# Maximum products on the array's row halves, and expert rows added back while the last tiles run

## The chip, the cores and the metric

The kernel runs on one core of a Trainium2 chip. The metric is the device time of one execution in microseconds (us), as the median of three runs. TensorE (PE) multiplies, with its weight loads shown as PEld; VectorE (DVE), ScalarE (ACT) and GpSimd (POOL) work on vectors; SyncE (SP) only issues DMAs here.

## The reference

One decoder layer over 1,024 tokens of width 1,024, in float32: RMSNorm, one input projection, three groups of attention heads side by side, the output projection, and a mixture of experts, then a last RMSNorm.

```
s_cmp = einsum(qh, k_cmp) * scale - slopes * dist_c      # C: compressed blocks, 8 heads
o_slc: softmax over selected blocks (16 of 16: causal)   # X: 8 heads
o_win: softmax over a band of 512 keys                   # Y: 8 heads
s = qh.kh * scale + (cum[q] - cum[k])                    # F: forgetting heads, 4
attn = p[:, :, 0] - lam_full * p[:, :, 1]                # D: differential heads, 4 x 2 maps
x = x + concat(o_a, o_b, o_c) @ w_out
eid = grp * EXPERTS_PER_GROUP + top_idx                  # two experts for each token
out = out + (silu(h @ w_gate[e]) * (h @ w_up[e]) * gate[:, e]) @ w_down[e]    # e = 0..31
return rmsnorm(x + out, norm_final)
```

## The kernel before

**Projection.** 16 groups of 128 columns are projected transposed, each value split in a high and a low half in fp32r, and the halves are stored in DRAM as `T_d`. This stage is the first 300 us.

**Attention.** `Plan` makes 36 units: for each of eight heads X, C, Y, then four F, then eight D. A unit's score matrix is cut in pieces of one block of 128 keys by up to four blocks of queries. Time is cut in 123 slots. A slot of PE holds up to three pieces of scores (`scores`), three maximum products of a later unit (`max_pass`, six slots ahead), at some slots the transpose of a row of shifts (`shift_T`), and the value products (`values`) of the slot before. A maximum product multiplies a block of queries by up to four blocks of keys, in one matmul over all 128 rows of the array: for X, Y and F the upper 64 rows hold the low half of q against the same k. DVE takes the maximum of each row of it (`maxima`); the maxima, negated, go back over SP's queue as one more row of the operand `Q2` (`shift_row`), so that the exponential of the scores can't overflow. Three PSUM banks take turns for the maximum products. In F units a piece on the diagonal gets a second small matmul (`identr` by `trimr`) that masks it. Value products load 64 columns of weights at a time, onto the two column halves of the array.

SP loads a unit's operands with `load_unit`: six DMAs for X, Y and F (64 rows of `T_d` each) and six of 32 rows for D. It does so two full units ahead, once the unit before has ended its scores (`s_ready`), since the buffers take turns. Between these, from the ninth full unit on, SP also writes seven blocks of zeros to `Y_d` (`zero_rows`, the rows of expert tiles that aren't run), and from the fifth on it loads the output weights (`wraw`).

**Experts.** 34 tiles of 96 token rows (32 experts and two tiles of overflow) run one after the other. In the round of tile n PE does the up product of n, the transposes of n+1, and the down product of n-1. DVE does `m_gate(n)` (with the copy `m_x(n+1)` of the transposed rows inside it), then `m_out(n-1)`. ACT stores each tile's result to `Y_d`. The weights take turns in five buffers; a tile's load is issued when the tile five before it has ended.

**End.** When all tiles are stored, POOL gathers for each of eight blocks of tokens its first and its second expert's row from `Y_d` (16 indirect DMAs, L921), DVE adds them weighted (L1775), takes the roots (`k_roots`, L1760 to L1766), and scales the rows (`k_final`, L1769); SP stores them (L749).

Of the kernel before, what the change touches and what calls it, by code (L numbers as in the profile page):

```python
# [24 lines left out]
P = 128  # L25
NT = SEQ // P
KC = D // P
HD = 64
# [14 lines left out]
NROWS = NTILES * CAP  # L43
# [20 lines left out]

class Unit:
# [6 lines left out]
    def __init__(self, kind, head, u=0):  # L72
# [6 lines left out]
        self.m = []  # L79
        for t in range(NT):  # L80
            for c, k in enumerate(range(lo(t), t + 1, 4)):
                self.m.append((t, c, k, min(4, t + 1 - k)))
# [16 lines left out]
class Plan:  # L99
# [4 lines left out]
    def __init__(self):  # L104
# [28 lines left out]
        early[0].m_use, early[0].tp_use = list(range(12)), 12  # L133
# [67 lines left out]
def program(nc, a, out):  # L201
# [5 lines left out]
    with ctx:  # L207
# [93 lines left out]
        identr, trimr = (at(n, [P, P], f32r, ZB + 60 * KB + 512 * k) for k, n in enumerate(("identr", "trimr")))  # L301
        pt = at("pt", [P, 6, 512], f32, ZE + 12 * KB)
# [4 lines left out]
        zrow = at("zrow", [P, D // 4], f32, ZE + 32 * KB)  # L307
# [24 lines left out]
        slf, shi, slo = (ri(n, [P, 2, NT]) for n in ("slf", "shi", "slo"))  # L332
# [30 lines left out]
        y1 = at("y1", [P, NT, D], f32, ZD)  # L363
        y2 = at("y2", [P, NT, D], f32, ZD + 32 * KB)
        gfin = at("gfin", [P, D], f32, ZC)
# [10 lines left out]
        Y_d = nc.dram_tensor("Y_d", [NROWS, D], f32).ap()  # L376
# [65 lines left out]
        yz_st = sem("yz_st")  # L442
# [43 lines left out]
        ovf_y = sem("ovf_y")  # L486

# [13 lines left out]
        ZERO = 7  # L501
        ROUTES = ((0, 4, "0"), (4, 6, "1"), (6, 8, "2"))
        A_BATCH = ((0, 1), (1, 1), (2, 2), (4, 4))
        K_BATCH = ((0, 3), (3, 3), (6, 1), (7, 1))

        class Events:
# [8 lines left out]
            def did(self, name, ins, eng=None):  # L515
# [3 lines left out]
                if eng is not None:  # L519
# [6 lines left out]
                    + [n + "v" for n in gelu_d] + ["dg1", "dg2", "kc2k", "dg3", "dg4", "dg5", "dg6", "dg7"]  # L526
# [6 lines left out]
                       "cj", "ej", "ejc", "nov", "info", "ids_ov"])  # L533
# [18 lines left out]
        def _(sp_):  # L552
# [54 lines left out]
            def load_unit(x):  # L607

                if x.kind == "D":
                    q0, k0 = (HD * x.head + g * P + 32 * x.u for g in (G_QD, G_KD))  # L610
                    for b, (qp, kp_) in enumerate(((0, 0), (1, 0), (0, 1))):
                        for dst, part, r0 in ((Q2, qp, q0), (K2, kp_, k0)):
                            sp_.dma_start(dst[x.set][32 * b:32 * b + 32, :].bitcast(f32), T_r[part, r0:r0 + 32, :])\
                               .then_inc(ld_in[x.set], 16)
# [5 lines left out]
                for dst, half, part, r0 in ((Q1, 0, 0, q0), (Q1, 1, 1, q0), (K1, 0, 0, k0), (K1, 1, 0, k0),  # L620
# [24 lines left out]
            for x in PLAN.units[:2]:  # L645
                shift_row(x)
# [553 lines left out]
        def _(dve):  # L1200
# [1106 lines left out]
```

## Time and profile before

| what | value |
|---|---|
| three runs | 1213.35, 1215.21, 1217.25 us |
| median | 1215.21 us |
| span of the profiled execution | 1207.4 us |
| granted TensorE clock, mean | 0.962 |
| PE busy | 1099.9 us (91%) |
| DVE busy | 596.5 us (49%) |
| ACT busy | 381.1 us (32%) |
| DMA | 251.59 MB, mean 208 GB/s |

The span runs from the first to the last instruction of one execution that the profiler recorded; the timed runs are executions too, and hold what lies around the span. The median stands 7.8 us over the span. Matmuls are pipelined, so their single durations overlap, and the time that a row of them costs is read from start to start.

### The profile page before, as it was taken

Reading aid. Unit: us, or ns where it says so; the run is one execution under the profiler, and the core shown is the slowest. Engines: PE = TensorE matmul, PEld = TensorE weight load, DVE = VectorE, ACT = ScalarE, POOL = GpSimd, SP = SyncE. Lnnn points to the kernel's source line nnn. Section 1 sums busy time; section 2 is a strip of 40 time slices with the busy share of each in tenths; the row PEclk is TensorE's granted clock in tenths of the full one; section 3 lists DMA queues with packets and bytes.
Section 4 is the critical chain, followed back from the end, with each engine's and each line's share of the span. In section 5 each row is a group of like instructions: output and inputs, shape, how many; then the busy total and the mean of one; then the engine's idle time right before and its main releaser. Section 6 shows DMA issues by size and latency. Waiting matters only on the chain.

```text
span 1207.4 us, 29635 instructions
## 1 busy us (share of the span) xinstructions
PE 1099.9 (91%) x12090; PEld 898.5 (74%) x12090; DVE 596.5 (49%) x1584; ACT 381.1 (32%) x693; POOL 211.4 (18%) x460
## 2 busy tenths in 40 slices
PE   6999899999999999999999899959999999999930
PEld 5989788777788888888777688848777777776710
DVE  5341344224666666665685434474443433333338
ACT  6321112221555555544777122200111111111112
POOL 1030000000523332321484000010110000000031
PEclk9999999999999999999999899968999999999975
DMA  9020755371657887863421422169999999999656
GB/s 356 18 87 16 283 162 157 109 222 70 164 134 198 210 217 186 216 144 81 116 58 26 158 97 96 70 221 360 385 380 373 405 376 374 385 384 370 225 179 267
DMA packets 69431, 251.59 MB, mean 208 GB/s; under 512 B 22225, under 2 KB 30321, under 8 KB 59441
## 3 DMA queue, kind: packets, MB, share of 16 engines
q1 hardware_dynamic: 59376, 219.54, 54.3%
q0 software_dynamic: 6112, 16.79, 4.2%
q10 hardware_dynamic: 3808, 13.37, 2.9%
q8 instruction: 98, 1.61, 0.6%
q14 instruction: 37, 0.30, 0.1%
HBM read 205.34 MB, written 49.15 MB: 211 GB/s over the span
## 4 chain that ended last, share of the span: by engine, by line
PE 75%; DMA 10%; DVE 6%; issue 3%; POOL 2%; ACT 1%; SPq 1%; POOLq 0%; DVEq 0%; ACTq 0%
PE PS L2153 13%; PE PS L1829 12%; PE PS L2007 9%; PE PS L2161 8%; PE PS L2089 7%; PE PS L1818 6%; DMA wdn<-in_wdn 5%; PE PS L1985 4%; PE PS L1946 4%; PE PS L1986 3%; PE PS L2144 2%; DMA wst<-in_wt 1%; DMA k<-T_d 1%; PE PS L1864 1%; PE PS L1979 1%
## 5 line engine op out<-in xcount | busy, mean ns | idle before, releaser
L2153 PEld LDWEIGHTS PS<-XT,wgu 128*64 128x64 f32 x4352 | 185.7, 140 | 33.6 <-issue 32.3
L1090 ACT ACTIVATE pt<-PS,cst 128x512 f32<-128x512 f32 (+3 forms) x288 | 167.2, 650 | 108.5 <-PE PS L1986 82.6
L2153 PE MATMUL PS<-XT,wgu 128*64 128x96 f32 x4352 | 192.2, 250 | 7.6 <-issue 5.1
L1398 DVE CUSTOM_DVE_ANT_0 junkm<-PS,cst 128x512 f32<-128x512 f32 (+3 forms) x276 | 133.5, 531 | 77.5 <-PE PS L1946 75.4
L2007 PEld LDWEIGHTS PS<-V,pt 128*64 128x64 f32 x3840 | 121.7, 138 | 22.5 <-issue 10.4
L2007 PE MATMUL PS<-V,pt 128*64 128x65 f32 x3840 | 137.4, 225 | 0.1
L2161 PE MATMUL PS<-wdn,aT 128*96 128x512 f32 x272 | 122.7, 593 | 1.0 <-DVE YO L1723 0.9
L1829 PE MATMUL PS<-hTh,wth 128*128 128x512 f32 x256 | 102.7, 401 | 4.5 <-DVE wtl L1245 4.5
L1829 PE MATMUL PS<-hTh,wtl 128*128 128x512 f32 x256 | 100.6, 393 | 0.0
L1829 PE MATMUL PS<-hTl,wth 128*128 128x512 f32 x256 | 100.3, 392 | 0.0
L1709 DVE TENSOR_SCALAR ge<-PS 128x192 f32<-128x192 f32 x34 | 12.2, 358 | 164.3 <-PE PS L2153 164.3
L823 POOL TENSOR_SCALAR_AFFINE_SELECT pt<-pt 128x128 f32<-128x128 f32 x224 | 64.2, 292 | 163.2 <-ACT pt L1090 120.8
L897 POOL DMA_INDIRECT XG<-h_d,ids x34 | 32.7, 963 | 296.7 <-PE PS L2144 283.2
L2161 PEld LDWEIGHTS PS<-wdn,aT 128*96 128x96 f32 x272 | 41.7, 163 | 56.4 <-issue 56.3
L1946 PE MATMUL PS<-k,q 128*128 128x128 f32 (+3 forms) x324 | 79.9, 348 | 1.6 <-DMA k<-T_d 1.3
L1985 PE MATMUL PS<-q,k 128*128 128x512 f32 (+1 forms) x228 | 81.2, 370 | 0.0
L1986 PE MATMUL PS<-q,k 65*128 65x512 f32 (+1 forms) x240 | 76.4, 339 | 0.0
L1154 ACT ACTIVATE ge<-ge 128x192 f32<-128x192 f32 x34 | 12.3, 363 | 193.1 <-DVE ge L1709 193.1
L1946 PEld LDWEIGHTS PS<-k,q 128*128 128x128 f32 (+1 forms) x324 | 56.7, 191 | 10.1 <-DMA k<-T_d 1.9
L1829 PEld LDWEIGHTS PS<-hTh,wth 128*128 128x128 f32 x256 | 48.5, 190 | 15.7 <-DVE wtl L1245 5.1
L1829 PEld LDWEIGHTS PS<-hTl,wth 128*128 128x128 f32 x256 | 48.5, 190 | 10.8 <-issue 1.0
L988 ACT ACTIVATE thi<-PS,cst 128x512 fp32r<-128x512 f32 x32 | 21.8, 686 | 109.1 <-PE PS L1829 88.5
(275 smaller groups left out, 1654.8 us busy)
## 6 DMA issues: line engine op xcount, KB each, us to landing
wgu<-in_wgu SPq DMA_DIRECT2D x34, 2048.0 KB, 14.0
wdn<-in_wdn SPq DMA_DIRECT2D x34, 1024.0 KB, 23.7
q<-T_d SPq DMA_DIRECT2D x58, 256.0 KB, 4.3
k<-T_d SPq DMA_DIRECT2D x58, 256.0 KB, 5.4
Y_d<-YO ACTq DMA_DIRECT2D x34, 384.0 KB, 10.1
wst<-in_wt SPq DMA_DIRECT2D x16, 512.0 KB, 6.6
T_d<-thi SPq DMA_DIRECT2D x16, 512.0 KB, 2.6
T_d<-tlo SPq DMA_DIRECT2D x16, 512.0 KB, 3.9
```

The lines of the kernel that those rows point to most:

```text
L823: ins = nc.gpsimd.affine_select(out=o, in_=o, compare_op=ALU.is_ge, fill=0.0, base=0, pattern=[[1, P]], channel_multiplier=-1)
L1090: ins = nc.scalar.activation(pt[:, (n + 2) % 6, 0:nt * P], PS[:, n % 3, 0:nt * P], ACT.Exp, scale=C("slopes", h, h + 1), bias=C("kb", w, w ...
L1398: V_.tensor_tensor_reduce(out=junk_[:, 0:L], in0=PS[:, bank, 0:L], in1=tab, scale=1.0, scalar=-3e38, op0=ALU.add, op1=ALU.max, accum_out=m ...
L1818: ins = mm(o, x[:, k, t * P:(t + 1) * P], wv[w][:, k, :], start=(k == 0 and x is hTh and w == 0), stop=(k == KC - 1 and w == 1))
L1829: ins = mm(PS[:, 2 * p + h, :], w[:, p, k * P:(k + 1) * P], x[:, k, h * 512:(h + 1) * 512], start=(k == 0 and w is wth and x is hTh), stop ...
L1946: ins = mm(PS[:, bank, 0:nk * P], q_[:, t * P:(t + 1) * P], k_[:, k0 * P:(k0 + nk) * P], start=True, stop=True)
L1985: mm(o, k1[:, j * P:(j + 1) * P], q1[:, q], start=True, stop=False)
L1986: ins = mm(o, k2[0:HD + 1, j * P:(j + 1) * P], q2[0:HD + 1, q], start=False, stop=True)
L2007: ins = mm(PS[h * HD:(h + 1) * HD, O_BANK[b % 2], (t % 4) * VW:(t % 4 + 1) * VW], pt[0:rows, (n + 2) % 6, q * P + h * HD:q * P + (h + 1) * ...
L2089: ins = mm(PS[:, 2 + h, :], x[:, t % 2, k, :], w[:, k, h * 512:(h + 1) * 512], start=(k == 0 and x is oth and w is woh), stop=(k == KC - 1 ...
L2153: ins = mm(PS[h * HD:(h + 1) * HD, 2 + p, f * CAP:(f + 1) * CAP], wgu[q][:, c, lo:lo + HD], XT[:, p, c, :], start=(c == 0 and f == 0), sto ...
L2161: ins = mm(PS[0:CAP, 5 + h, :], aT[:, p, c, :], wdn[q][:, c, h * 512:(h + 1) * 512], start=(c == 0), stop=(c == 1))
```

## The change

It has two parts.

1. The maximum products of all units but the first X, the first Y and the C units run as 64-row tiles. The high half of q against the high half of k stands on the lower 64 rows (`Q1`, `K1`) and once more on the upper 64 (`Q1`, `K2`; for D `Q2`, `K2`). The planner gives each product a side so that the sides' loads are even, and the order of the pieces within a unit is a table. The zero rows and the row of shifts of `Q2` move to the lower half, and `scores` multiply over 128 rows. A D unit is loaded with ten DMAs. The C units' mask is multiplied over 65 rows.
2. The experts 7, 15, 23 and 31 are run last (`TILE`), and their rows stored apart (`Z_d`). POOL gathers the rows of the other thirty tiles while the last four run (16 indirect DMAs that leave out rows out of bounds), DVE adds them between its work on tiles 31 to 33 and after it (`early_rows`), and behind the last tile only eight gathers from `Z_d` and eight additions remain. The slot numbers for this are worked out in the second round (`last_rows`). `zero_rows` goes; the load of the last norm's weights moves ahead of the experts.

```diff
+FINAL = tuple(range(7, NE, 8))
+TILE = tuple(e for e in range(NE) if e not in FINAL) + tuple(range(NE, NB)) + FINAL
+EARLY = NB - len(FINAL)
+CAUSAL = ((3, 0), (0, 0), (2, 0), (4, 0), (4, 1), (6, 1), (5, 0), (1, 0), (5, 1), (6, 0), (7, 0), (7, 1))
...
+            load = [0, 0]
             for x, k in self.m_at.get(t, ()):
+                side = load[1] < load[0]
+                x.side = [*(x.side if k else []), None if x.kind == "C" or x.n == 2 else side]
+                load[side] += 0 if x.kind == "C" else x.m[k][3]
...
                 if x.kind == "D":
-                    for b, (qp, kp_) in enumerate(((0, 0), (1, 0), (0, 1))):
-                        for dst, part, r0 in ((Q2, qp, q0), (K2, kp_, k0)):
+                    for dst, at_, part, r0 in ((Q1, 0, 0, q0), (Q1, 32, 1, q0), (K1, 0, 0, k0), (K1, 32, 0, k0),
+                                               (Q2, 64, 0, q0), (Q2, 96, 1, q0), (K2, 64, 0, k0), (K2, 96, 0, k0),
+                                               (Q2, 32, 0, q0), (K2, 32, 1, k0)):
...
-                if f in range(8, 8 + ZERO):
-                    zero_rows(f - 8)
...
+            pool.wait_ge(dve_did, DV.of("slot_a"))
+            for p in range(2):
+                pool.wait_ge(y_st[p], 16 * EARLY // 2 + 1)
+            for i in range(2 * NT):
+                if i in (0, 6):
+                    pool.wait_ge(m_dn, EARLY + (i > 0))
+                if i >= 12:
+                    pool.wait_ge(e_add, i - 11)
+                pool.indirect_dma_start(
+                    out=ye[i % 12][:], out_offset=None, in_=Y_d,
+                    in_offset=bass.IndirectOffsetOnAxis(ap=slot_a[:, i % 2, i // 2:i // 2 + 1], axis=0),
+                    bounds_check=YROWS - 1, oob_is_err=False).then_inc(ye_in[i % 12], 16)
...
             for t in range(NT):
-                for k, dst in enumerate((y1, y2)):
...
+                pool.indirect_dma_start(
+                    out=zt[:, t, :], out_offset=None, in_=Z_d,
...
+            def early_rows(*steps):
+                for i in steps:
+                    t, k = i // 2, i % 2
+                    dve.wait_ge(ye_in[i % 12], 16 * (i // 12 + 1))
+                    V_.scalar_tensor_tensor(out=x2[:, t, :], in0=ye[i % 12][:], scalar=wa[:, k, t:t + 1],
+                                            in1=x2[:, t, :], op0=ALU.mult, op1=ALU.add).then_inc(e_add, 1)
+                    dve.wait_ge(e_add, i + 1)
...
             for n in range(NB):
                 m_gate(n)
                 if n:
                     m_out(n - 1)
+                if n == 1:
+                    last_rows()
+                if n == EARLY + 1:
+                    early_rows(0, 1, 2)
+                if n == EARLY + 2:
+                    early_rows(*range(3, 11))
             m_out(NB - 1)
+            early_rows(*range(11, 16))
...
+            dve.wait_ge(ovf_add, 15 * n_ovf + 1)
             for t in range(NT):
-                dve.wait_ge(k_in[t], 32)
-                for k, y in enumerate((y1, y2)):
-                    V_.scalar_tensor_tensor(out=x2[:, t, :], in0=y[:, t, :], scalar=w12[:, k, t:t + 1],
...
+                dve.wait_ge(k_in[t], 16)
+                V_.scalar_tensor_tensor(out=x2[:, t, :], in0=zt[:, t, :], scalar=wf[:, t:t + 1],
+                                        in1=x2[:, t, :], op0=ALU.mult, op1=ALU.add).then_inc(k_acc, 1)
...
                 t, c, k0, nk = x.m[k]
-                q_, k_ = (q2[0:96], k2[0:96]) if x.kind == "D" else (q1[:], k1[:])
+                lower, upper = slice(0, HD), slice(HD, P)
+                if x.side[k] is None:
+                    q_, k_ = q1[:], k1[:]
+                elif x.side[k] == 0:
+                    q_, k_ = q1[lower], k1[lower]
+                else:
+                    q_, k_ = (q2 if x.kind == "D" else q1)[upper], k2[upper]
```

On PE, in a slot of X scores, this stood before: two matmuls for each piece of scores (L1985, L1986), three maximum products (L1946) and the value products (L2007).

```order
L1985 MATMUL PS<-q1_3_109,K1y_124 128x384
L1986 MATMUL PS<-q2_0_110,k2_0_118 128x384
L1946 MATMUL PS<-k1_1_115,q1_1_107 128x512
L1946 MATMUL PS<-k1_1_115,q1_1_107 128x256
L1946 MATMUL PS<-k1_1_115,q1_1_107 128x512
L2007 MATMUL PS<-vcm_78,pt_131 64x65 x16
```

In the changed kernel the same place of PE's order reads as follows (`k1` is the lower half, `k2` the upper).

```order
L2117 MATMUL PS<-q1_3_109,K1y_124 128x384
L2118 MATMUL PS<-q2_0_110,k2_0_118 128x384
L2078 MATMUL PS<-k1_1_115,q1_1_107 128x512
L2078 MATMUL PS<-k2_1_119,q1_1_107 128x256 x2
L2139 MATMUL PS<-vcm_78,pt_132 64x65 x16
```

One product of 512 columns stands on the lower side and the two others on the upper one, where before all three used all rows.

In a slot with an F unit's maximum products, PE's order before has the masks (L1949) between them.

```order
L1946 MATMUL PS<-k1_0_114,q1_0_106 128x128
L1949 MATMUL PS<-trimr_130,identr_129 128x128
L1946 MATMUL PS<-k1_0_114,q1_0_106 128x256
L1949 MATMUL PS<-trimr_130,identr_129 128x128
L1946 MATMUL PS<-k1_0_114,q1_0_106 128x384
L1949 MATMUL PS<-trimr_130,identr_129 128x128
L1957 MATMUL PS<-cst_49,sh_63 8x128
L2007 MATMUL PS<-V_81,pt_131 64x65 x14
```

In the changed kernel PE's order there is this.

```order
L2078 MATMUL PS<-k1_0_114,q1_0_106 128x512
L2081 MATMUL PS<-trimr_130,identr_129 128x128
L2078 MATMUL PS<-k2_0_118,q1_0_106 128x128
L2081 MATMUL PS<-trimr_130,identr_129 128x128
L2078 MATMUL PS<-k2_0_118,q1_0_106 128x384
L2081 MATMUL PS<-trimr_130,identr_129 128x128
L2089 MATMUL PS<-cst_49,sh_63 8x128
L2139 MATMUL PS<-V_81,pt_132 64x65 x14
```

The masks still use all 128 rows, and stand between products that now use 64.

## Rows read from the trace of the kernel before

**Rows 1.** Windows: stretch, its us, busy of each engine, clock, DMA share, GB/s.
```profile
302.00:400.00 98.00, 95.37 (x1323) 80.02 (x1322) 64.14 (x259) 54.46 (x95) 35.47 (x88) 1.00 0.68 171
...
480.00:555.00 75.00, 74.14 (x1018) 63.39 (x1017) 47.95 (x189) 38.27 (x69) 19.34 (x56) 1.00 0.66 162
...
600.00:662.00 62.00, 57.95 (x965) 46.28 (x965) 44.52 (x161) 45.90 (x74) 40.37 (x76) 1.00 0.20 50
```
**Rows 2.** Instructions of L1946 after the first two units; PE's idle time ended by loads.
```profile
L1946 PE MATMUL PS<-k,q x312: 220/344/632, 313.1 to 648.3; 128*128 128x512 f32 x72, 96*128 96x512 f32 x32, 128*128 128x128 f32 x18, 128*128 128x384 f32 x18
...
  DMA k<-T_d: 3.2, 4
```
**Rows 3.** Timeline of PE in an X/Y slot: start us, us, instructions.
```profile
459.73 0.80 PE L1946 MATMUL PS<-k,q 128*128 128x384 f32 x3
460.46 0.92 PE L2007 MATMUL PS<-V,pt 128*64 128x65 f32 x24
461.31 0.39 PE L1985 MATMUL PS<-q,k 128*128 128x256 f32 x1
461.53 0.28 PE L1986 MATMUL PS<-q,k 65*128 65x256 f32 x1
461.65 0.22 PE L1985 MATMUL PS<-q,k 128*128 128x128 f32 x1
```
**Rows 4.** Timeline of PE: fp32r products, then f32 transposes, both on the whole array.
```profile
765.74 0.39 PE L2089 MATMUL PS<-wol,oth 128*128 128x512 f32 x1
765.97 0.39 PE L2089 MATMUL PS<-woh,otl 128*128 128x512 f32 x1
766.20 1.04 PE L2059 MATMUL PS<-cst,h 128*128 128x128 f32 x8
```
**Rows 5.** Chain of waits at one load of an X unit: start us, us, what.
```profile
361.05 7.61 DMA k<-T_d
```
**Rows 6.** Timeline at a D unit's load: SP's first issue, PE's first use, PE's wait.
```profile
598.33 0.30 SPq L613 DMA_DIRECT2D q<-T_d  x1
...
606.05 0.57 PE L1946 MATMUL PS<-k,q 96*128 96x128 f32 x3
607.41 0.27 PE L1957 MATMUL PS<-cst,sh 128*8 128x128 f32 x1 [0.79 <-DVE mx L1398]
```
**Rows 7.** DMA issues, 598 to 602 us and 1125 to 1126 us: KB, us to landing.
```profile
k<-T_d SPq DMA_DIRECT2D x3, 128.0 KB, 2.9
...
Y_d<-YO ACTq DMA_DIRECT2D x1, 384.0 KB, 8.5
```
**Rows 8.** Timeline, last tiles: DVE's clamps and copy, PE's last products.
```profile
1139.72 0.36 DVE L1709 TENSOR_SCALAR ge<-PS 128x192 f32<-128x192 f32 x1 [4.75 <-PE PS L2153]
...
1142.19 0.56 DVE L1696 COPY XT<-PS 128x384 f32<-128x384 f32 x1
...
1143.86 5.50 PE L2153 MATMUL PS<-XT,wgu 128*64 128x96 f32 x128
...
1149.40 0.36 DVE L1709 TENSOR_SCALAR ge<-PS 128x192 f32<-128x192 f32 x1 [4.75 <-PE PS L2153]
...
1153.84 3.64 PE L2161 MATMUL PS<-wdn,aT 128*96 128x512 f32 x8 [0.87 <-DVE YO L1723]
```
**Rows 9.** Timeline, the end: gathers, additions, roots, last scaling.
```profile
1162.28 0.96 POOL L921 DMA_INDIRECT y<-Y_d,slot  x1 [39.38 <-DMA Y_d<-YO]
...
1169.30 2.60 DVE L1775 SCALAR_TENSOR_TENSOR x<-y,w,x 128x1024 f32<-128x1024 f32 x2 [11.10 <-DMA y<-Y_d,slot]
...
1182.81 1.01 POOL L921 DMA_INDIRECT y<-Y_d,slot  x1 [0.30 <-issue]
1182.92 0.16 DVE L1760 TENSOR_SCALAR nv<-ssq 128x3 f32<-128x3 f32 x1
...
1200.49 3.68 DVE L1769 SCALAR_TENSOR_TENSOR y<-x,rstd,gfin 128x1024 f32<-128x1024 f32 x3
```
**Rows 10.** Windows: PE's clock in the stretch after PE had idled 3.57 us.
```profile
142.54:145.95 3.41, 3.41 (x9) 2.64 (x8) 2.23 (x5) 1.06 (x1) 0.00 (x0) 0.50 0.76 304
```

More of the change, by code:

```diff
@@ L132, in __init__ @@
         self.end = slot + self.DEEP + 2
-        early[0].m_use, early[0].tp_use = list(range(12)), 12
+        early[0].m_use, early[0].tp_use, early[0].side = list(range(12)), 12, [None] * 12
         early[1].m_use, early[1].tp_use = [13], 14
@@ L361, in program, with late @@
                for q, o in enumerate((ZE, ZD + 16 * KB, ZD + 40 * KB, ZB + 48 * KB, ZC + 16 * KB))]
-        y1 = at("y1", [P, NT, D], f32, ZD)
-        y2 = at("y2", [P, NT, D], f32, ZD + 32 * KB)
-        gfin = at("gfin", [P, D], f32, ZC)
+        zt = at("zt", [P, NT, D], f32, ZD)
+        ye = [at(f"ye{b}", [P, D], f32, (ZC if b < 6 else ZE) + 4 * KB * (b % 6)) for b in range(12)]
+        dead = (4 * COL["dist"][0] + 31) // 32 * 32
+        gfin = at("gfin", [P, D], f32, dead)
+        _do = [dead + 4 * D]
+        def late(name, shape, dt=f32):
+            n = 4
+            for s in shape[1:]:
+                n *= s
+            t = at(name, shape, dt, _do[0])
+            _do[0] += (n + 31) // 32 * 32
+            assert _do[0] <= 4 * COL["distc"][1]
+            return t
+        lm, am, wa, wl, sf, zf, sd, eq, ew, es = (
+            late(n, [P, 2, NT]) for n in ("lm", "am", "wa", "wl", "sf", "zf", "sd", "eq", "ew", "es"))
+        wf, wd, zs, sj = (late(n, [P, NT]) for n in ("wf", "wd", "zs", "sj"))
+        slf, shi = late("slf", [P, 2, NT]), late("shi", [P, 2, NT])
+        slot_a = late("slot_a", [P, 2, NT], u32)
+        slot_f, slot_j = late("slot_f", [P, NT], u32), late("slot_j", [P, NT], u32)
+        jt = late("jt", [P, 1])
         junk3 = at("junk3", [P, D], f32, ZB + 60 * KB)
@@ L375, in program @@
         h2_d = nc.dram_tensor("h2_d", [SEQ, D], f32).ap()
-        Y_d = nc.dram_tensor("Y_d", [NROWS, D], f32).ap()
+        Y_d = nc.dram_tensor("Y_d", [YROWS, D], f32).ap()
+        Z_d = nc.dram_tensor("Z_d", [ZROWS, D], f32).ap()
+        V_d = nc.dram_tensor("V_d", [CAP, D], f32).ap()
         def sem(n):
@@ L486, in program @@
         ovf_y = sem("ovf_y")
+        ovf_g = sem("ovf_g")
+        ovf_add = sem("ovf_add")
+        ye_in = [sem(f"ye_in{b}") for b in range(12)]
+        e_add = sem("e_add")
         k_in = [sem(f"k_in{t}") for t in range(NT)]
@@ L640, in _ @@
             for half in range(2):
[L641 removed]
+                sp_.dma_start(K1y[HD * half:HD * half + HD, :].bitcast(f32), T_r[half, G_KW * P:G_KW * P + HD, :])\
                    .then_inc(ky_in, 16)
@@ L644, in _ @@
             store_t(14, 0)
-            for x in PLAN.units[:2]:
-                shift_row(x)
+            shift_row(PLAN.units[0])
             store_t(15, 1)
@@ L1103, in _ @@
                     copy(identr[:], ident)
+                    copy(picks[0:HD, :], ident[0:HD])
+                    copy(picks[HD:HD + 1, :], ones[HD:HD + 1, :])
                     copy(trimr[:], C("tris"), scale=NEG).then_inc(trim_set, 1)
@@ L1908, in loaded @@
             def loaded(x):
-                f = PLAN.full.index(x)
-                return 96 * ((f - 1) // 3 + 1) - 64 * (x.set < 2) if f else 96
+                before = sum(160 if y.kind == "D" else 96 for y in PLAN.full if y.set == x.set and y.n <= x.n)
+                return before - (64, 80, 0, 0)[x.set]
             def operands(x):
```

213 lines of the change are left out of this document (135 added, 78 removed).

## The prediction

> **What bounds the kernel now.** I read the windows first: in the stretches of X, Y and F units PE is busy 97 to 99% of the time, in that of the D units 93%, with DVE at 72%, ACT at 74% and POOL at 65% [rows 1]. A busy PE may hold waits, so I read the timeline of a slot next. PE's rows follow each other there without a gap and at their own pace, so a slot's length is the sum of PE's starts, and PE bounds X, Y and F. In the D stretch the timeline shows PE standing 0.79 us for DVE's maxima before a transpose [rows 6]: there PE is one of several engines that are nearly full. The chain of waits holds a second bound: the load of an X unit's operands, 7.61 us from its last issue to its landing, with PE's first maximum product right behind it [rows 5]; such waits cost 3.2 us in all [rows 2], so they are a limit just reached. The experts are bound by PE and the weights' stream, and the change leaves both as they are up to the last four tiles. The end, from PE's last product (starts 1153.84, 3.64 long [rows 8]) to the end of the span at 1207.4, is 49.9 us without PE.
>
> **Part 1, the maximum products.** From start to start 512 columns take 0.23 [rows 4] and 256 columns 0.12 (461.53 to 461.65 [rows 3]), so in proportion 384 take 0.175; a single block I put at 0.11, hardly less than 256 columns, as an estimate. The planner puts one product of 512 on the lower side and the two smaller ones (512 columns between them) on the upper. If the sides run at the same time, every such slot saves what lies on one side, 0.23 us; a slot with 512, 512 and 512 saves one of them, 0.23 again. A unit has four slots, so 0.93 us. Seven X and seven Y units: 13.0 us. The four F units: a mask over the whole array stands behind most products, so only three slots have two products side by side, which saves 0.11, 0.12 and 0.23, 0.46 a unit, 1.9 us in all. The eight D units: 7.5 us on PE, but DVE and ACT are nearly full there, so I take 0 to 3 of it.
>
> What it adds is the change of the array's form. PE now goes from the whole array (scores) to the row halves (maxima) to the column halves (values), where it went from the whole to the column halves. No row shows row halves. The nearest is the change to column halves: the three products L1946 of rows 3 would take 0.175 + 0.23 + 0.23 = 0.64, and the next row starts 0.73 after the first, so 0.09 is lost going in. Coming back the first product of 256 columns takes 0.22 (461.31 to 461.53) against the 0.12 of the next, 0.10 lost, which is a weight load that could not run ahead. That it is the form and not the number type is shown by rows 4: fp32r product to f32 transposes on the whole array costs 0.23 (765.97 to 766.20), the pace of the product before it. So a step into row halves costs between 0 and 0.20 (0.09 + a load of 128 columns, 0.11); I take 0.09, the row's own drain, because the change into column halves stands nearest to it. Steps added: one for each of 56 slots of X and Y, and two more in each of seven pairs where a transpose over the whole array follows, 70; in F the masks force the way back: 6, 4, 4 and 2 in a unit's four slots, 64; in D 5 a unit, 40.
>
> Sum: X and Y 13.0 - 70 x 0.09 = 6.7 gained; F 1.9 - 64 x 0.09 = 3.9 lost; D: on PE 7.5 - 40 x 0.09 = 3.9 gained, of which the full engines leave 0 to 2. D also gets four more DMAs for each unit. Their issues follow each other by 0.42 to 0.47 on SP (598.33 to 600.95 for six), so the last goes out 1.9 us later: 598.33 + 2.6 + 1.9 + 2.9 to landing [rows 6, 7] = 605.7, and PE needs them at 606.05. Cover 0.3 us; where a slot gets shorter it is gone, so I book the whole D stretch as 1 lost to 1 gained, 0 taken. The removed zero rows only give bandwidth to the loads of X and Y, whose windows shrink with the slots; I book these two against each other. Part 1: 2.8 us gained; at a step of 0, 13.0 + 1.9 less about 3 for loads that then come late (the chain shows them just in time), 12 gained; at 0.20, X and Y 1.0 lost, F 10.9 lost, D 2 lost: 14 lost.
>
> The Trainium skill bears on this: "TensorEngine Tiling (Array Packing)", Key Properties, says that changing the tiling mode (not just the tile) drains the engine. By that rule the step isn't 0, and the trace's 0.09 for the column halves agrees with it. Its "TensorE: Matmul & The Clock Gate", Part 3, says that small products on distinct row groups run at the same time; no row here shows it.
>
> **Part 2, the end.** The roots' small work in the second round (22 operations of 0.16 [rows 9] and a gap each, some 4.5 us) lies in DVE's 4.75 us of idle time before a clamp [rows 8], and the copy that PE waits for has 1.1 us to spare behind it; I put it at nothing, and at a few tenths if the cover is short. The gathers behind the last tile go from 16 to 8: before they start every 1.25 us, 1162.28 to 1182.81 and the first additions follow 7.0 after the first start [rows 9]. Now: first addition 7.0 less about 1.2 (it needs one gather, not two) = 5.8 after the first gather's start. Then DVE alone: 8 additions, 8 scalings of 1.28 and 3 sets of roots, each five operations of 0.16 with their gaps, about 1.1, = 23.8. Then 3.2 from the last scaling's end (1204.17) to the span's end. From the first gather's start 32.8, before 45.1: 12.3 less.
>
> Against it stands DVE. The 16 early additions of 1.28 us are 20.5 us, and DVE has 4.75 us of room in a round. POOL's early gathers wait for the store of tile 29, issued between 1125 and 1126 and 8.5 to landing [rows 7], so 1134; the first starts near 1134.8 and its rows are there at about 1140, the third's at 1143. But `early_rows(0, 1, 2)` stands in DVE's queue behind the work on tile 30 and ahead of `m_gate(32)`, which before starts at 1139.72 [rows 8]: it starts at 1144.4, 4.7 late. Behind it are queued the copy `m_x(33)`, 1142.19 before and with 1.1 us to spare before PE's up product of 1143.86: PE starts 3.7 late. Then eight additions, 10.2 us, stand ahead of `m_gate(33)`: from about 1149 to 1159, instead of 1149.40. The last down product follows 4.4 after `m_gate(33)` begins, so 1163.5 instead of 1153.84, 9.7 later. PE stands idle for some 5 us before it; after an idle of 3.57 us the trace shows the clock at 0.5 of 2.4 GHz, 1.2, for 3.41 us [rows 10], which would add up to 1.7 to a product of 3.6. The other five additions end before the gathers land. Part 2: 12.3 - 9.7 = 2.6 gained, 0.9 with the slow clock; I take 2. Bounds: if the early rows land by 1136, DVE's own 14 us of additions in two rounds of 4.75 idle still delay by about 5: 7 gained; with landings as late as 9 us, as under the full stream, and the slow clock, 3 lost.
>
> **Sum.** 2.8 + 2 = 4.8 gained. Profiled span 1207.4 - 4.8 = 1202.6, and with the 7.8 us between the span and the median of the runs, 1210.4.
>
> **Rivals.**
> A. The step into row halves costs next to nothing (all form changes between halves hidden by weight loads that run ahead): 12 + 2 = 14 gained, 1201. For it: most of PE's loads run ahead of their products. Against: the 0.09 of rows 3.
> B, the slower side. Each step costs its drain and an exposed load, 0.20, as in and out of the column halves together: 14 lost, 2 gained, 1227. The place is F above all: 64 steps in 16 slots, 10.9 us. It decides from 0.11 a step on (13.0 + 1.9 + 2 against 134 steps and half of D's 40). For it: the pair of values in rows 3, and that the load can't run ahead is just what the way back shows. Against: the first load may be issued during the drain.
> C. The two sides don't run at the same time, or the planner's sides don't do what they say: the 13.0 and 1.9 are not there and 134 steps of 0.09, 12, are lost: 1225. Against: the value products on the column halves come every 35 ns (24 in 0.85 [rows 3]), where 64 columns of weights at the single block's 0.11 for 128 would take 0.055 one after the other.
> D. The end doesn't stall at all, since gathers land earlier: 7 gained there, with part 1 as forecast, 1205.
>
> **How the numbers follow.** Forecast as summed 0.37, of itself 1204 to 1217; A 0.27; B 0.20; C 0.05; D 0.11. A measurement of this kernel tells 0.3%, 3.6 us, from no change. Faster by more: 0.6 of the forecast's chance, all of A and D: 0.58 with a bit off for ends that go wrong together, 0.54. Within 0.3%: 0.35 of the forecast's and a few hundredths of A and B, 0.18. Slower: B, C and the rest, 0.28. The range takes in A and most of B: 1196 to 1226.
>
> **What would show it.** Right: in X and Y slots the maximum products (now L2078) of both sides start within some 0.01 us of each other, and the time from them to the values falls by about 0.14; F slots get longer by 0.2 to 0.3 each; D's slots stay. In the end, `m_gate(33)` starts near 1159 less what part 1 gained, the last product 10 us later behind the last up product's start than before, and 33 us lie between the first `Z_d` gather and the end. Wrong: F slots that don't lengthen (A), X and Y slots longer than before (B), starts of the sides one behind the other (C), no wait of the down product for DVE (D).

## The result, and the profile after

The changed kernel takes 1246.22 us (median of four runs, 1240.17 to 1248.96), the kernel before 1214.28 beside it: a ratio of 1.0272, with a 95% interval from 1.0244 to 1.0301. It is 32 us slower, where 4.8 us of gain were forecast. Its profiled span is 1245.8 us at a mean clock of 0.952, against 1207.4 at 0.962, so the two profiles differ by 38.4 us.

Where they lie is read from the starts of PE's rows. The kernel computes the maxima of 28 full units (all but the C units), numbered here from 1 in their order; the starts of each unit's first maximum product cut both spans at the same places of the program. The table gives the us between such starts, of the two kernels and of all experiments that the text comes to. "Early" is from unit 3 to unit 6, then come the rest of X and Y (11 units), F (4), D (7 of the 8), the experts from the first up product to that of tile 32 (counting from 0 in the order in which the tiles run), and the end from there.

| kernel | early | X/Y | F | D | experts | end | span |
|---|---|---|---|---|---|---|---|
| before | 42.5 | 149.7 | 52.9 | 82.1 | 320.1 | 73.2 | 1207.4 |
| after | 54.4 | 155.5 | 60.5 | 87.7 | 319.4 | 80.9 | 1245.8 |
| tiles_alone | 48.0 | 155.5 | 60.5 | 90.9 | 323.4 | 73.3 | 1241.3 |
| tail_alone | 43.0 | 151.9 | 53.1 | 81.1 | 321.6 | 82.0 | 1218.3 |
| small_first | 49.9 | 151.9 | 60.5 | 87.6 | 319.8 | 80.9 | 1237.5 |
| skip_loop | 50.4 | 156.5 | 60.5 | 92.9 | 319.5 | 73.8 | 1242.4 |
| row_first | 42.6 | 153.1 | 62.1 | 89.2 | 319.2 | 99.1 | 1255.5 |
| f_whole | 49.5 | 152.4 | 52.5 | 88.0 | 318.3 | 98.3 | 1248.3 |
| one_side | 45.7 | 156.3 | 61.9 | 82.9 | 319.7 | 98.5 | 1253.6 |
| tiles_fixed | 42.2 | 155.0 | 52.6 | 84.7 | 322.2 | 73.2 | 1217.4 |
| before_again | 42.8 | 150.0 | 52.8 | 83.7 | 320.0 | 72.7 | 1210.7 |
| tail_late | 42.8 | 152.4 | 52.9 | 82.6 | 321.3 | 81.5 | 1219.3 |
| tail_late_2 | 42.2 | 150.1 | 52.9 | 82.2 | 319.4 | 65.2 | 1199.4 |
| tail_spread | 43.0 | 152.0 | 52.6 | 80.7 | 319.1 | 65.2 | 1198.0 |

So the 38.4 us are 11.9 early, 5.8 in X/Y, 7.6 in F, 5.6 in D and 7.7 at the end; the small rest cancels. The experts in between lose nothing. (The ends of row_first, f_whole, one_side and tail_late hold a disturbance of their occasion, shown with tail_late.)

Each row is a single profile, and where PE's program in a stretch is the same, rows still differ: in the six profiles with the attention of before by 0.8 us early, 2.7 in X/Y, 0.5 in F and 3.0 in D, and among after, tiles_alone and skip_loop by 6.4 early, 1.0 in X/Y and 5.2 in D. Much of this is the clock, which falls in some of these profiles and not in others. So F and the end can mostly be read to 1 us, the other columns only to a few us.

**A slot.** The timeline of a slot (start us, us, instructions, in brackets the idle time before and what ended it) answers to [rows 3]. The three products of 512, 128 and 384 columns now take 0.56 us together. The kernel before had pieces of 128, 256 and 384 columns in this place of a unit, and they took 0.62:
```profile
465.66 0.62 PE L1946 MATMUL PS<-k,q 128*128 128x128 f32 x3
...
466.42 0.27 PE L1957 MATMUL PS<-cst,sh 128*8 128x128 f32 x1
```
The changed kernel:
```profile
481.62 0.27 PE L2118 MATMUL PS<-q,k 128*128 128x128 f32 x1
...
481.82 0.56 PE L2078 MATMUL PS<-k,q 64*128 64x512 f32 x3
...
482.36 0.69 DVE L1461 CUSTOM_DVE_ANT_0 junkm<-PS,cst 128x512 f32<-128x512 f32 x1 [1.17 <-PE PS L2078]
...
483.21 0.27 PE L2089 MATMUL PS<-cst,sh 128*8 128x128 f32 x1 [0.83 <-DVE mx L1461]
483.41 1.04 PE L2139 MATMUL PS<-V,pt 128*64 128x65 f32 x28
```
The three starts lie at 0, 4 and 170 ns: both sides do run together (one_side below has the time on one side alone). But the row to see is L2089, the shift transpose of the unit ahead. It writes the bank of this slot's first product, and DVE must have taken that product's maximum. Before, the first piece had 128 columns; the new order of pieces puts 512 columns first, whose maximum takes 0.69 and begins later. The transpose starts 1.39 after the first product, where it was 0.76 before (465.66 to 466.42). The waits of PE from 370 to 597 us (what, us in total, times, longest) say how often:
```profile
PE PS L2089 <- DVE mx L1461: 9.1, 11, 0.8
```
The kernel before has no such wait in the same stretch.

**The clock early.** Windows of the changed kernel (columns as in [rows 1]):
```profile
316.30:330.00 13.70, 12.96 (x83) 9.68 (x83) 4.88 (x20) 5.25 (x8) 5.13 (x9) 0.50 0.49 116
330.00:350.50 20.50, 18.32 (x276) 14.82 (x273) 11.83 (x46) 10.17 (x19) 6.72 (x18) 1.00 0.41 92
350.50:357.30 6.80, 6.41 (x50) 4.70 (x52) 2.52 (x11) 1.74 (x3) 0.49 (x2) 0.50 0.06 9
```
The granted clock is 0.5 (1.2 GHz) in 20.5 us of a stretch where the kernel before had 2.4 GHz throughout [rows 1]. Right ahead of the first of them PE stands three times within four us:
```profile
313.35 0.55 PE L2078 MATMUL PS<-k,q 64*128 64x512 f32 x3 [0.50 <-DMA k<-T_d]
314.73 0.27 PE L2089 MATMUL PS<-cst,sh 128*8 128x128 f32 x1 [0.83 <-DVE mx L1461]
317.04 0.79 PE L2113 MATMUL PS<-maskc,picks 65*128 65x512 f32 x1 [1.07 <-DMA maskc<-shra]
```
The last wait is for a row that SP now issues behind eight loads. The second fall, from 350.5, is in no other profile, tiles_alone and skip_loop with the same instructions included.

**F.** An F slot of the changed kernel:
```profile
557.25 0.50 PE L2078 MATMUL PS<-k,q 64*128 64x512 f32 x2
557.68 0.33 PE L2081 MATMUL PS<-trimr,identr 128*128 128x128 f32 x1
557.94 0.44 PE L2078 MATMUL PS<-k,q 64*128 64x384 f32 x1
558.30 0.33 PE L2081 MATMUL PS<-trimr,identr 128*128 128x128 f32 x1
558.56 1.04 PE L2139 MATMUL PS<-V,pt 128*64 128x65 f32 x28
```
From a mask (L2081, whole array) to the next product on a half 0.26 us pass, from that product to the next mask 0.36. The whole-array rows of the same slot stand with f_whole below.

**The end.** The chain of waits of the changed kernel (start us, us, what) answers to [rows 8, 9]:
```profile
1155.70 9.13 DMA Y_d<-YO
...
1165.76 8.21 DMA ye<-Y_d,slot_a
1173.99 1.28 DVE x L1827
...
1182.25 1.21 DVE x L1827
...
1192.73 0.37 DVE ge L1772
...
1196.68 5.36 PE PS L2293 x8
...
1207.94 1.30 DVE x L1827
1209.26 0.55 DVEq L1846
...
1220.48 5.58 DVE x L1905 x5
```
It is the stall that was forecast: additions ahead of the clamp at 1192.73, then the last product, for 3.4 us of it at 1.2 GHz (5.36 long, before 3.64). What was not forecast is the row at 1209.26: DVEq is DVE's own instruction stream. There it reads the number of overflow tiles, and from 1210.2 to 1220.3 it walks 19 steps of the loop over them, 0.53 us each, and none is taken. The rows of the first gather, issued at 1206.82 and 4.5 us under way, had been there since 1211.3.

### The profile page after: what moved, and what is told of

Its sections match the earlier page's. It is cut to its first block, busy times and chain, and to the rows that moved or that the text cites. A ratio compares the mean times of both kernels' runs of the same rounds, so it can differ in the third digit from the quotient of the medians.

```text
span 1245.8 us, 29740 instructions
## 1 busy us (share of the span) xinstructions
PE 1118.8 (90%) x12090; PEld 891.7 (72%) x12090; DVE 611.6 (49%) x1609; ACT 382.0 (31%) x695; POOL 224.8 (18%) x470
## 3 DMA queue, kind: packets, MB, share of 16 engines
q1 hardware_dynamic: 53504, 216.26, 52.6%
## 4 chain that ended last, share of the span: by engine, by line
PE 77%; DVE 9%; DMA 6%; issue 4%; SPq 2%; ACT 1%; DVEq 0%; POOL 0%; POOLq 0%; ACTq 0%
PE PS L2285 14%; PE PS L1955 12%; PE PS L2293 9%; PE PS L2139 9%; PE PS L2221 7%; PE PS L1944 6%; PE PS L2117 4%; PE PS L2078 4%; PE PS L2118 3%; PE PS L2276 2%; DVE x L1827 2%; DMA wst<-in_wt 1%; DMA q<-T_d 1%; PE PS L1990 1%; PE PS L2111 1%
## 5 line engine op out<-in xcount | busy, mean ns | idle before, releaser
L2139 PE MATMUL PS<-V,pt 128*64 128x65 f32 x3840 | 140.4, 228 | 0.9 <-issue 0.9
L2139 PEld LDWEIGHTS PS<-V,pt 128*64 128x64 f32 x3840 | 124.5, 141 | 20.7 <-issue 8.7
L2293 PE MATMUL PS<-wdn,aT 128*96 128x512 f32 x272 | 125.9, 606 | 3.8 <-DVE YO L1786 3.8
L2293 PEld LDWEIGHTS PS<-wdn,aT 128*96 128x96 f32 x272 | 42.6, 167 | 61.5 <-issue 56.8
L2117 PE MATMUL PS<-q,k 128*128 128x512 f32 (+1 forms) x228 | 80.7, 369 | 0.0
L2118 PE MATMUL PS<-q,k 128*128 128x512 f32 (+1 forms) x240 | 77.0, 341 | 0.0
L2078 PE MATMUL PS<-k,q 64*128 64x512 f32 (+1 forms) x324 | 69.9, 417 | 3.9 <-DMA k<-T_d 3.0
L2078 PEld LDWEIGHTS PS<-k,q 64*128 64x128 f32 (+1 forms) x324 | 35.9, 189 | 32.5 <-issue 18.9
L1955 PEld LDWEIGHTS PS<-hTh,wtl 128*128 128x128 f32 x256 | 48.4, 189 | 10.4
```

What stands on the lines that cost most here:

```text
L1955: ins = mm(PS[:, 2 * p + h, :], w[:, p, k * P:(k + 1) * P], x[:, k, h * 512:(h + 1) * 512], start=(k == 0 and w is wth and x is hTh), stop ...
L2078: ins = mm(PS[:, bank, 0:nk * P], q_[:, t * P:(t + 1) * P], k_[:, k0 * P:(k0 + nk) * P], start=True, stop=True)
L2117: mm(o, k1[:, j * P:(j + 1) * P], q1[:, q], start=True, stop=False)
L2118: ins = mm(o, k2[:, j * P:(j + 1) * P], q2[:, q], start=False, stop=True)
L2139: ins = mm(PS[h * HD:(h + 1) * HD, O_BANK[b % 2], (t % 4) * VW:(t % 4 + 1) * VW], pt[0:rows, (n + 2) % 6, q * P + h * HD:q * P + (h + 1) * ...
L2293: ins = mm(PS[0:CAP, 5 + h, :], aT[:, p, c, :], wdn[q][:, c, h * 512:(h + 1) * 512], start=(c == 0), stop=(c == 1))
```

## The experiments

The runs came in three groups on one chip, on three occasions, with runs of the kernel before in each. That kernel took 1211.29 in the first, 1224.48 in the second (13 runs, 1215.84 to 1231.72) and 1211.57 in the third; so ratios are compared, and stretches of the profiles.

**tiles_alone and tail_alone**: the two parts apart.
```diff
 # tiles_alone: kernel before, with CAUSAL/BANDED, Unit.m, x.side, load_unit, shift_row,
 #   augment, kc1/kc2, picks, max_pass and scores of the change
 # tail_alone: kernel before, with FINAL/TILE, last_rows, early_rows, Z_d/V_d, ye/zt of the change
```


> The kernel before with part 1 alone (tiles on the array's halves, their operands, the new order of the pieces); its end stays as before. By the two traces the changed kernel is 31.4 us behind when the first up product of the experts starts and the rest is lost at the end. Theory: all of the 31.4 comes from part 1, so 1214 + 31 = 1245 us, within 3. Rival 1, my forecast for part 1 (2.8 gained): 1211. Rival 2: the removed zero rows and the other loads of part 2 have a share in the 31.4: 1230 to 1240.

> The kernel before with part 2 alone (rows gathered early, the last four experts' rows apart); its maximum products stay on the whole array. Theory: from the start of up product 32 to the end the changed kernel needs 80.9 us where the kernel before needs 73.2, so 7 to 8 lost: 1222 us. Rival, my forecast for part 2 (2 gained): 1212.

Measured: 1241.68, ratio 1.0244 (1.0205 to 1.0284), and 1220.01, ratio 1.0083 (1.0051 to 1.0115). Against the kernel before of their group they lose 30.4 and 8.7, where 31.4 and 7 to 8 were expected, so both theories held within some 1 us. Each part is a loss by itself. Together they lose 39, a little more than the 32 of the whole change, so nothing is left over for the removed zero rows (rival 2 of tiles_alone).

**small_first**: the first two pieces change places.
```diff
-CAUSAL = ((3, 0), (0, 0), (2, 0), (4, 0), (4, 1), (6, 1), (5, 0), (1, 0), (5, 1), (6, 0), (7, 0), (7, 1))
-BANDED = ((3, 0), (0, 0), (2, 0), (4, 0), (4, 1), (1, 0), (5, 0), (5, 1), (6, 1), (6, 0), (7, 0), (7, 1))
+CAUSAL = ((0, 0), (3, 0), (2, 0), (4, 0), (4, 1), (6, 1), (5, 0), (1, 0), (5, 1), (6, 0), (7, 0), (7, 1))
+BANDED = ((0, 0), (3, 0), (2, 0), (4, 0), (4, 1), (1, 0), (5, 0), (5, 1), (6, 1), (6, 0), (7, 0), (7, 1))
```


> The changed kernel with one edit: the first slot of a unit computes the piece of 128 columns ahead of the one of 512, so that the bank which the shift transpose needs is free after a maximum of 0.29 us and not of 0.69 us. Theory: the transpose behind 22 of the first slots starts 1.38 us after the first product, where it was 0.76 before; each gives back about 0.55, 12 us in all, and with shorter idle times the clock stays up between 316 and 330 us, up to 7 more: 1246 - 12 to 19 = 1227 to 1234. Rival, the wait is the array's change of form from row halves to the whole, and the order has nothing to do with it: 1246, and the transpose still 1.2 after the last product.

Measured: 1241.03, ratio 1.0233 (1.0193 to 1.0273). In its timeline the transpose starts 0.81 after the first product:
```profile
477.24 0.55 PE L2078 MATMUL PS<-k,q 64*128 64x128 f32 x3
477.60 0.29 DVE L1461 CUSTOM_DVE_ANT_0 junkm<-PS,cst 128x128 f32<-128x128 f32 x1 [0.97 <-PE PS L2078]
...
478.05 0.27 PE L2089 MATMUL PS<-cst,sh 128*8 128x128 f32 x1 [0.26 <-DVE mx L1461]
```
The mechanism is as the theory had it, 0.57 for each transpose and not a change of form. The size was too high: X/Y gets 3.6 back and not 6.3 (11 times 0.57), since two waits for loads now stand there, 1.8 together where it was one of 0.7, and the clock is at half for 3.4 us from 379.8. D gets nothing, since other waits take its place, and the clock still falls from 318.4 to 332.0.

**row_first**: small_first, and the late row ahead of two loads.
```diff
             load_unit(PLAN.full[2])
-            load_unit(PLAN.full[1])
             for p in range(2):
                 sp_.wait_ge(t_st[p], 32 * 8 + 1)
             shift_row(PLAN.units[1])
+            load_unit(PLAN.full[1])
```


> small_first with one more edit: the shift row of the first C unit is issued ahead of the two loads of the first Y unit, and not behind them. In the profiles of tiles_alone, small_first, skip_loop and of the changed kernel the first score of that unit waits 0.97 to 1.68 us for this row, and the granted clock is at 0.5 for 7 to 14 us from about that point on. Theory: the wait goes, the clock stays at 1.0 there, and the stretch between the maxima of the 3rd and 6th full unit (50.0 us in small_first, 42.5 before) falls to 43 to 44: 7 to 8 less than small_first, 1233 us. Rival: the clock falls for another reason (the transpose's wait, the power of tiles on both halves): only the wait of 1.7 goes, 1239.

Measured: 1251.15 in the second group, ratio 1.0208 (1.0136 to 1.028), too wide to tell 7 us. The profile tells it: early falls from 49.9 to 42.6, what it was before. A row and a window of small_first, then a window of row_first:
```profile
318.86 0.79 PE L2113 MATMUL PS<-maskc,picks 65*128 65x512 f32 x1 [1.68 <-DMA maskc<-shra]
```
```profile
318.40:332.00 13.60, 13.14 (x83) 9.68 (x83) 4.79 (x19) 5.36 (x8) 5.05 (x9) 0.50 0.53 116
```
```profile
316.00:359.00 43.00, 41.89 (x592) 33.38 (x592) 29.76 (x116) 23.32 (x42) 18.92 (x44) 1.00 0.58 130
```
So a wait of 1.7 us, beside others, cost 7: the rest was the clock. Whether such a wait is enough to bring the clock down is taken up with one_side.

**f_whole**: small_first, F's products on the whole array.
```diff
-                x.side = [*(x.side if k else []), None if x.kind == "C" or x.n == 2 else side]
+                x.side = [*(x.side if k else []), None if x.kind in "CF" or x.n == 2 else side]
```


> small_first with the maximum products of the four F units on the whole array (128 rows, high and low part of k). A unit F takes 15.35 us there and 13.2 before; by the accounts of PE's starts a step from row halves to the mask costs 0.19, and one back 0.19. Theory: the form's changes cost it all, F falls back to 13.2, and the time by 8.4, to 1232 to 1233. Rival, F is longer for its loads or for the order of its pieces: no change, 1241.

Measured: 1250.31, ratio 1.0198 (1.0123 to 1.0273), again in the second group. F falls from 60.5 to 52.5, 8.0 back, as expected. A slot like the one shown above:
```profile
533.09 0.51 PE L2078 MATMUL PS<-k,q 128*128 128x512 f32 x2
533.43 0.27 PE L2081 MATMUL PS<-trimr,identr 128*128 128x128 f32 x1
533.54 0.39 PE L2078 MATMUL PS<-k,q 128*128 128x384 f32 x1
533.77 0.22 PE L2081 MATMUL PS<-trimr,identr 128*128 128x128 f32 x1
533.92 1.04 PE L2139 MATMUL PS<-V,pt 128*64 128x65 f32 x28
```
From mask to product it is 0.11 and to the next mask 0.23, where the halves took 0.26 and 0.36; the slot's maxima take 0.83 instead of 1.31.

**one_side**: small_first, all 64-row products on the lower half.
```diff
-                x.side = [*(x.side if k else []), None if x.kind == "C" or x.n == 2 else side]
+                x.side = [*(x.side if k else []), None if x.kind == "C" or x.n == 2 else 0]
```


> small_first with every 64-row product on the lower half: as many steps between forms, no two products at the same time. Theory: side by side saves 0.93 us a unit X or Y at most and 0.6 by the account of the starts (in D 0.9), so 8 to 13 us are lost for X and Y, about 2 for F, and 0 to 7 for D where other engines are nearly full: 1251 to 1262. Rival C of the forecast, the sides give nothing: 1241.

Measured: 1259.06, ratio 1.0305 (1.0223 to 1.0387), too wide for the parts, which the profile tells. X/Y loses 4.4, 0.40 a unit where 0.6 to 0.93 were expected, F 1.4, and D gains 4.7. The theory's sign for D was wrong. The two largest waits of PE in the D stretch, first of the changed kernel, then of one_side (us in total, times, longest):
```profile
PE PS L2089 <- DVE mx L1461: 6.6, 7, 1.3
PE PS L2078 <- DMA k<-T_d: 2.5, 4, 1.0
```
```profile
PE PS L2089 <- DVE mx L1461: 1.4, 3, 0.6
PE PS L2078 <- DMA k<-T_d: 0.9, 3, 0.5
```
So in D maxima that come two at a time gain nothing, and PE waits longer. The clock falls more often as well: to 0.5 twice for 3.4 us in the changed kernel (from 647.4 and 661.1), three times in small_first, once in the kernel before (from 589.7), never from 232 to 696 us in one_side. All six profiles with D on two sides took 87.6 to 92.9 there, the two on one side 82.9 and 84.7. That it is DVE, nearly full in D, that can't take two maxima at once fits these waits, but is argued.

one_side has the late row of the early stretch too, for the edit of row_first is not in it. Two rows and a window of it:
```profile
316.02 0.78 PE L2078 MATMUL PS<-k,q 64*128 64x128 f32 x3 [0.75 <-DMA k<-T_d]
...
319.73 0.50 PE L2113 MATMUL PS<-maskc,picks 65*128 65x512 f32 x1 [1.67 <-DMA maskc<-shra]
```
```profile
316.00:361.70 45.70, 43.95 (x590) 34.88 (x590) 29.91 (x115) 22.46 (x40) 18.73 (x43) 1.00 0.54 121
```
PE waits 2.4 us here, and 2.2 in small_first (0.29, 0.26 and 1.68), yet the clock stays at 2.4 GHz, and early takes 45.7 and not 49.9. The five profiles in which the clock fell early have both the late row and two products at a time. With one of them gone (row_first and tiles_fixed, or one_side) it stayed up. So the wait alone does not bring the clock down; one_side also takes away the transpose's wait of 0.26, and which of the two counts is not shown.

The first of these rows also gives the time on one side: products of 128, 512 and 384 columns take 0.78 there, and 0.55 in small_first.

**tiles_fixed**: tiles_alone with all four losses undone.
```diff
 # CAUSAL and BANDED as in small_first, the shift row as in row_first
-                x.side = [*(x.side if k else []), None if x.kind == "C" or x.n == 2 else side]
+                x.side = [*(x.side if k else []), None if x.kind in "CF" or x.n == 2 else 0 if x.kind == "D" else side]
```


> Part 1 alone (tiles_alone) with its four losses undone as the runs so far name them: the piece of 128 columns first, the shift row of the first C unit ahead of two loads, the F units' maxima on the whole array, the D units' maxima on one half only (no two at a time). From the stretches measured: from the third full unit's maxima to the sixth's 42.6 (before 42.5), X and Y 152 to 153 (149.7), F 51.8 (52.3), D 58.0 (58.8). Theory: the sum is 2 to 4 us above the kernel before, 1.002 to 1.003 of it, where tiles_alone had 1.0244. Rival: the losses overlap or move elsewhere (loads of D, clock): 8 us or more above it.

Measured: 1223.77, ratio 1.0089 (1.0057 to 1.012). Early, F and the end are those of before. X/Y, at 155.0, is 5 above it, of which up to 3.4 are the clock, at 0.5 from 372.2 to 379.0; D is 2.6 above. So 19 of the 30 us came back, not 27: the theory lost to its rival. What is left of part 1, tiles side by side for X and Y and on one side for D, is still no gain. The starts of PE's rows in X/Y say why: steps (4.1) and transposes that still come later (1.8) take what the products save (6.4).

**skip_loop**: the changed kernel, DVE's loop within a condition.
```diff
+            with dve.If(0 < n_ovf):
                 with dve.Fori(0, MAX_OVF - SURE) as j:
```


> The changed kernel with one edit: VectorE's loop over overflow tiles (19 steps, none of them taken here, 0.53 us each, 1210.2 to 1220.3 us) stands within a single condition, so that it is stepped over when there is none. Theory: the loop, not the gathered rows, holds the last additions back: the rows of the first gather landed at 1211.36, the first addition starts at 1220.48. It starts 9 us earlier and the time falls by 8 to 9 to 1237 to 1238. Rival, the end is bound by the gathers and by VectorE's own work: 1246, within 1.

Measured: 1238.62, ratio 1.0209 (1.0179 to 1.0239), 7.6 less than the changed kernel by the ratios, where 8 to 9 were expected. The first addition now waits for the gather, and comes 8.95 after the last copy, where it took 18.4:
```profile
1206.56 0.69 DVE L1786 COPY YO<-PS 96x512 f32<-96x512 f32 x1 [6.16 <-PE PS L2294]
1207.16 6.55 DVE L1827 SCALAR_TENSOR_TENSOR x<-ye,wa,x 128x1024 f32<-128x1024 f32 x5
1215.51 2.48 DVE L1906 SCALAR_TENSOR_TENSOR x<-zt,wf,x 128x1024 f32<-128x1024 f32 x2 [1.80 <-DMA zt<-Z_d,slot_f]
```

**tail_late**, **tail_late_2** and **tail_spread**: tail_alone with the condition of skip_loop, and the additions moved into DVE's idle time.
```diff
-                if n == EARLY + 1:
+                if n == EARLY + 2:
                     early_rows(0, 1, 2)
-                if n == EARLY + 2:
-                    early_rows(*range(3, 11))
+                if n == EARLY + 3:
+                    early_rows(3, 4)
             m_out(NB - 1)
-            early_rows(*range(11, 16))
+            early_rows(*range(5, 16))
 # tail_spread besides: gathers 5 to 15 wait for m_dn of EARLY + 2 (before: gather 6, EARLY + 1)
```


> tail_alone with two edits: VectorE's overflow loop is stepped over by one condition when nothing overflows, and the early additions stand where VectorE waits anyway: three behind the copy out of tile 31, two behind that of tile 32, eleven behind that of tile 33. Theory: PE's last product starts as early as in the kernel before (20 us behind up product 32), 11 additions of 1.3 end 38.6 behind that start, then 8 additions, 8 scalings and three sets of roots, 23.8, and 3.2 to the end: 66, where the kernel before needs 73.2: 7 less than before, 1204 to 1205. Rival: the last eleven additions and the queue of the gathers take back what they save (landings of 8 us, slow clock in the last tile): within 2 of the kernel before, 1210 to 1213.

> tail_late once more, on another occasion. If the bursts of tile 32's products belong to the kernel, the time stays near 1221, at or above the kernel before; if they belong to the occasion, it is 7 below the kernel before of this group (1204 to 1206 where that takes 1211 to 1213).

> tail_late with one edit: only the first five gathers are issued while tile 32's up products run, the other eleven wait for the down product of tile 31 (their rows are needed from 24 us behind that start on). Theory: the full stream of gathers is what slows PE in tile 32; with five under way the stretch is shortened to at most some 5 us of bursts, or none, and the time is 5 to 9 under tail_late's where tail_late has the bursts (1212 to 1216 against 1221), equal to it where not. Rival: the number of gathers in flight does not matter: as tail_late.

> The kernel before, unchanged, for its profile beside the others of this group: in the second group of runs it took 1224 us, in the first 1211. In tail_late PE's products of tile 32 came in bursts of 3 to 5 with 0.3 to 1.5 us between them for 14 us while twelve gathers were under way. Theory 1: such bursts need the gathers, and this profile shows none; a time above 1211 then sits elsewhere, and this profile says where. Theory 2: the bursts come in any kernel in some executions: they are seen here too.

Measured: tail_late 1221.9 in the second group, ratio 0.9982 (0.9953 to 1.0012); on the third occasion the same kernel 1201.05, ratio 0.9913 (0.9897 to 0.993), and tail_spread 1201.21, 0.9924 (0.9903 to 0.9945); before_again 1212.4. The end takes 65.2, where 66 were expected and the kernel before needs 73.2:
```profile
1134.23 5.50 PE L2261 MATMUL PS<-XT,wgu 128*64 128x96 f32 x128
...
1143.91 5.50 PE L2261 MATMUL PS<-XT,wgu 128*64 128x96 f32 x128
...
1153.89 3.65 PE L2269 MATMUL PS<-wdn,aT 128*96 128x512 f32 x8 [0.87 <-DVE YO L1767]
```
```profile
1144.63 3.91 DVE L1808 SCALAR_TENSOR_TENSOR x<-ye,wa,x 128x1024 f32<-128x1024 f32 x3
...
1158.23 14.48 DVE L1808 SCALAR_TENSOR_TENSOR x<-ye,wa,x 128x1024 f32<-128x1024 f32 x11
1174.05 6.10 DVE L1887 SCALAR_TENSOR_TENSOR x<-zt,wf,x 128x1024 f32<-128x1024 f32 x5 [1.34 <-issue]
```
PE's last products stand where they stood before [rows 8], at the full rate. On this occasion it beats the kernel before by 10.5 us; on the second it was level with it (ratio 0.9982). There its end was 16 us longer, and the timeline and a window say where:
```profile
1143.06 0.37 PE L2261 MATMUL PS<-XT,wgu 128*64 128x96 f32 x3 [0.48 <-issue]
1144.47 0.39 PE L2261 MATMUL PS<-XT,wgu 128*64 128x96 f32 x4 [1.05 <-issue]
1145.89 1.04 PE L2261 MATMUL PS<-XT,wgu 128*64 128x96 f32 x5 [1.04 <-issue]
```
```profile
1140.00:1154.00 14.00, 5.92 (x48) 3.65 (x45) 0.00 (x0) 0.00 (x0) 9.82 (x10) 0.69 0.99 376
```
Tile 32's products come in bursts of at most five, with gaps that no semaphore explains, while the DMA engines, mostly with the gathers, are at 0.99. The four profiles of the second group (tail_late, row_first, f_whole, one_side) all have them in this tile, which is why their ends in the table are 16 to 18 us longer; no profile of the other groups has, before_again included. Since tail_late_2 shows that the same kernel can go without, the bursts belong to the occasion; since no bursts occurred in the third group, tail_spread could not show whether fewer gathers avoid them. Nor is it known where the kernel before left its 13 us in the second group, since no profile of it was kept there. This stays open.

## Why the prediction was wrong

Three steps failed above all. The sum of part 1 had no term for the new order of the pieces, and none for the row that moved behind eight loads; and in part 2 the first addition was put 5.8 us after the first gather, where it came 13.7 after. The forecast's own terms follow one by one.

- **Two products side by side save 0.93 us a unit.** Right in kind, too large. The starts from one maximum product to the next add up to 15.96 us over 11 units before and to 9.53 now, 0.58 a unit less; against one_side the sides are worth 0.40.
- **A step into row halves costs 0.09.** Right into the halves in X/Y: the mean time from the last score (or value product, in five slots) to the first maximum product goes from 0.201 to 0.295 over 44 steps. The count was short: a transpose stands behind a product on a half in each of the 11 units, not in one of two. Wrong in F, where the way back counts as well: product to mask 0.169 before and 0.363 now, mask to product 0.069 and 0.257, so 0.19 each way. The rule of the Trainium skill ("TensorEngine Tiling (Array Packing)", Key Properties: changing the tiling mode drains the engine) agrees with time lost in both directions. F lost 7.6, between the 3.9 of the forecast and the 10.9 of rival B, whose place and size of a step were the right ones; rival A, steps at next to nothing, is refuted. The 8.0 that f_whole gave back and the 1.4 that side by side is worth in F (one_side) make 0.15 for each of its 64 steps.
- **X/Y gain 6.7.** This step of the prediction failed. The 6.7 stood for 14 units: three of them are the stretch early, and 11 are X/Y. The sum had the products and the steps only; the change also orders the pieces anew, and the prediction left that out. The transpose that needs the bank of the first piece came 0.63 later behind the first product of every unit, and behind the last one 8.1 us in all over 11 units. Products saved 6.4, steps took 4.1, and X/Y lost 5.8. With the small piece first 6.3 of the 8.1 are gone (small_first).
- **Loads and SP's queue: nothing.** Failed. The queue that one row was moved behind was not priced: 1.07 us of wait, and with it the fall of the clock from 316.3. Early lost 11.9. It is 4.5 shorter in small_first, up to 3.4 of it for the second fall of the clock, and 7.3 shorter again with the row ahead of the loads (row_first).
- **D: 0.** Lost 5.6. The prediction capped the gain where DVE and ACT are nearly full; that it turns negative, since PE's waits grow and the clock falls, it did not see (one_side). PE's waits in the stretch sum to 10.5 us, before to 4.2; 2.5 of them are for loads, for which a cover of 0.3 was reckoned.
- **The end gains 2.** It lost 7.7, where the terms summed to 2.6. The stall was right in mechanism: `m_gate(33)` came 27.8 behind the start of up product 32 (forecast 24.8), since the early rows took 8.2 to land and not 5. The slow clock took the 1.7 that was named. And the step "first addition 5.8 after the first gather" failed: it came 13.7 after, for DVE still had its overflow loop to walk. In the kernel before DVE walks that loop too, to 1168.5, and the first two gathers' rows land at 1169.2, ahead of the addition at 1169.30 [rows 9]: it cost nothing. Five additions put ahead of it uncovered 9 us (skip_loop). From the first gather to the end it took 39.0, where 32.8 were forecast.
- Rivals C (sides not concurrent) and D (an end without stall) are refuted, C by the starts 4 ns apart, D by the chain.

## What to carry to other kernels

When an edit reorders pieces, follow each bank from its writer to its reader and to the next writer: the reader of a large piece that comes first holds up whatever reuses its bank. Small tiles pay only where several follow each other: between whole-array work each change of form cost 0.1 to 0.2 us here, in F far more than running side by side gave, in X and Y with the later transposes about as much. And before additions are put "where the engine is idle", look at what its own instruction stream does there: an idle engine may be walking a loop.

## What the runs showed of the hardware

- Products on the two row halves start 4 ns apart and run together: three of them (1,024 columns) take 0.55 us on two halves and 0.78 on one. Changing between halves and the whole array costs 0.09 (from scores) to 0.19 us (to and from a mask).
- PE's waits of 0.5, 0.8 and 1.1 us close behind each other (in small_first 0.3, 0.3 and 1.7), in a stretch where it was otherwise busy, went before 13.7 us at 1.2 GHz. With the last of them removed the clock stayed at 2.4 GHz and 7 us came back; but waits of 0.75 and 1.67 us left it at 2.4 GHz in one_side, where no products ran side by side.
- An empty step of a loop with a condition in it takes DVE 0.53 us; one condition around the loop replaces 19 of them.
- Indirect gathers of 128 rows of 4 KB took 5.7 to 8.2 us to land while many were in flight, and 2.9 to 4.5 when most of their rows were skipped.
- On one occasion PE's matmuls came in bursts beside such gathers, at a DMA share of 0.99, which drew out a row of 5.3 us to 19 to 23; why is open.
